# Recurrent mixer of a two-block model: head by head with the projections in between, instead of stage by stage

## The reference

```python
def hgrn2_mixer(x, lb, w_in, out_norm, w_o):
    proj = x @ w_in                                   # 1024 -> 4096
    q = silu(proj[..., :1024]); f = proj[..., 1024:2048]
    v = proj[..., 2048:3072];   gate = proj[..., 3072:]
    log_f = logaddexp(log(lb), log1p(-lb) + log_sigmoid(f))
    k = (1.0 - lb) * sigmoid(-f)
    # 8 heads of 128, chunks of 64 tokens; G = cumsum of log_f inside a chunk
    def step(state, chunk):
        inter = einsum('bhtd,bhde->bhte', qc * exp(G), state)
        decay = exp(where(causal, G[t] - G[s], -inf))
        A = einsum('bhtd,bhsd,bhtsd->bhts', qc, kc, decay)
        intra = einsum('bhts,bhse->bhte', A, vc)
        new_state = exp(G_last) * state + einsum('bhsd,bhse->bhde', kc * exp(G_last - G), vc)
        return new_state, inter + intra
    o = rms_norm_2(o, out_norm.reshape(H, DV))        # per head
    return (o * silu(gate)) @ w_o
```

## Time and profile before

| what | value |
| --- | --- |
| median of 3 runs | 3634.28 us (3632.82 to 18645.5) |
| the profiled execution's own time | 3637.17 us |
| its span, first to last instruction | 3635.4 us |
| PE busy | 3467.8 us (95%) |
| DVE, ACT, POOL busy | 1756.2 (48%), 754.0 (21%), 1944.4 us (53%) |
| mean granted PE clock | 0.969 |

### The profile page before, as it was taken

The page is one execution under the profiler, slowest core; times in us unless marked ns, Lnnn a source line. Parts: engine busy times, 40 slices in busy tenths (PEclk is TensorE's granted clock), DMA queues, the critical chain, the costliest instruction groups (busy, mean ns, idle before and its releaser), DMA issues. The chain is left out here.

```text
span 3635.4 us, 45543 instructions
## 1 busy us (share of the span) xinstructions
PE 3467.8 (95%) x15768; PEld 2738.6 (75%) x15768; DVE 1756.2 (48%) x3022; ACT 754.0 (21%) x1292; POOL 1944.4 (53%) x1172
## 2 busy tenths in 40 slices
PE   8998999999999999999999788899989999899998
PEld 4635788888888888888888556688767888588885
DVE  1043167768595657777775333423022856433203
ACT  2122122211112211111111232322022332222103
POOL 3403564555545566666666413466645652366663
PEclk9998999999999999999999979999999999899999
DMA  4431233535444475555554101222312200122231
GB/s 177 147 116 46 87 122 119 217 119 194 144 152 181 149 281 193 190 198 195 190 188 146 58 24 41 75 95 96 104 69 81 93 30 7 52 90 95 98 101 61
DMA packets 141137, 438.20 MB, mean 121 GB/s; under 512 B 13568, under 2 KB 13696, under 8 KB 136832
## 3 DMA queue, kind: packets, MB, share of 16 engines
q1 hardware_dynamic: 82512, 301.62, 24.2%
q10 hardware_dynamic: 58544, 135.55, 10.6%
HBM read 367.91 MB, written 69.21 MB: 120 GB/s over the span
## 5 line engine op out<-in xcount | busy, mean ns | idle before, releaser
L1757 POOL TENSOR_SCALAR whi<-ring 128x1024 fp32r<-128x1024 f32 x519 | 563.8, 1086 | 1585.8 <-issue 942.9
L1759 POOL TENSOR_TENSOR wlo<-ring,whi 128x1024 fp32r<-128x1024 f32 x519 | 1310.1, 2524 | 43.4
L364 PE MATMUL ps<-norm_hi,whi 128*128 128x512 f32 x1304 | 556.8, 427 | 14.1 <-DVE norm_lo L1186 13.0
L366 PE MATMUL ps<-norm_hi,wlo 128*128 128x512 f32 x1304 | 512.6, 393 | 0.0
L365 PE MATMUL ps<-norm_lo,whi 128*128 128x512 f32 x1304 | 511.0, 392 | 0.0
L364 PE MATMUL ps<-mixed_hi,whi 128*128 128x512 f32 x1024 | 398.4, 389 | 2.7 <-DVE mixed_lo L1488 2.7
L366 PE MATMUL ps<-mixed_hi,wlo 128*128 128x512 f32 x1024 | 398.4, 389 | 0.0
L365 PE MATMUL ps<-mixed_lo,whi 128*128 128x512 f32 x1024 | 398.3, 389 | 0.0
L1484 DVE TENSOR_TENSOR A<-A 128x512 f32<-128x512 f32 x128 | 353.9, 2765 | 22.8 <-DMA A<-gate_map 21.9
L364 PE MATMUL ps<-mix_hi,whi 128*128 128x512 f32 x768 | 303.7, 395 | 18.8 <-DVE mix_lo L1186 18.8
L365 PE MATMUL ps<-mix_lo,whi 128*128 128x512 f32 x768 | 302.1, 393 | 0.0
(11 more groups left out here) (332 smaller groups left out, 5231.8 us busy)
## 6 DMA issues: line engine op xcount, KB each, us to landing
ring<-stream SPq DMA_DIRECT2D x519, 512.0 KB, 3.3
gelu_map<-A ACTq DMA_DIRECT2D x128, 256.0 KB, 2.0
gate_map<-A ACTq DMA_DIRECT2D x16, 2048.0 KB, 11.7
A<-gelu_map ACTq DMA_DIRECT2D x128, 256.0 KB, 3.3
A<-gate_map ACTq DMA_DIRECT2D x32, 1024.0 KB, 6.0
A<-ada_w SPq DMA_DIRECT2D x12, 2048.0 KB, 8.2
X<-x_in SPq DMA_DIRECT2D x1, 2048.0 KB, 17.8
out<-X SPq DMA_DIRECT2D x8, 256.0 KB, 2.0
```

The lines of the kernel that those rows point to most:

```text
L364: first = mm(out_, lh, rh, start=start, stop=False)
L366: return first, mm(out_, ll, rh, start=False, stop=stop)
L1757: g.tensor_scalar(h[:], raw[:], 1.0, 0.0, ALU.mult, ALU.add).then_inc(whi_ready, 1)
L1759: g.tensor_tensor(rest[:], raw[:], h[:].bitcast(F32), ALU.subtract).then_inc(split_ready, 1)
```

## The change

The layer is rewritten as a loop over heads with three heads in flight. Turn i has the projections of head a = i, the pairs and states of head b = i-1, the output and norm of head c = i-2, and the gating of head d = i-3. A turn has eight slots on PE. In each stands half a product of head a, in the order forget gate, value, output gate, query, two slots for each; the weight columns are laid out to match. Values are now projected by feature and transposed on PE, like the decayed keys, both through bank 2.

The pairs of one head are no longer multiplied with the values level by level. DVE writes those of level 0 masked into a plane and merges those of the other levels and of the diagonal into the same plane by `copy_predicated`; then PE multiplies the plane with the values once per head. The states of a head are kept side by side (7 updates in a row, each waiting for the one before), and their products with the decayed queries are accumulated in the same bank, so that the addition on DVE is gone. The norm is made per head with a full sum by `ones`, a root and a reciprocal over 128x512, and no spread. POOL makes the gaps of a head between its splits. Planes, semaphores and the norm's bookkeeping follow (`HE` now has 12 buffers for the gaps; most others have two, by the parity of the head).

The core of the diff:

```diff
 # tensor
-            linear("hgrn_in", "x_hgrn", count=16)
-            by_token("hgrn_v", "x_hgrn", KC, PROD["hgrn_in"] + 16)
-            linear("hgrn_in", "x_hgrn", tiles="hgrn_gate", first=24, count=8)
...
+            def hgrn_linear(h, s):
+                part, half = divmod(s, 2)
+                t, p = FIRST["hgrn"] + 4 * h + part, PROD["hgrn"] + 4 * h + part
+                for k in range(4 * half, 4 * half + 4):
+                    if k == 0:
+                        tile_in(t)
+                        pe.wait_ge(bank_free, p + 1)
...
+            def hgrn_delta(h, odd):
+                if h:
+                    pe.wait_ge(state_ready, (NCH - 1) * h)
+                for c in range(odd, NCH - 1, 2):
...
+                    last = mm(ps[:, 3 + 2 * odd, w], A[r, HKT, w], A[r, HV + h % 2, w], start=True, stop=True)
+                last.then_inc(delta_ready, 1)
+            def hgrn_out(h):
+                pe.wait_ge(masked_ready, (LEVELS + 1) * (h + 1))
...
+                    mm(ps[:, 4, r], two(HV, h)[:, r], two(HMASK, h)[:, r], start=tb == 0, stop=False,
+                       skip_group_check=True)
+                for c in range(1, NCH):
+                    pe.wait_ge(state_ready, (NCH - 1) * h + c)
+                    r = slice(c * CH, (c + 1) * CH)
+                    last = mm(ps[:, 4, r], states(h, c - 1), two(HLF, h)[:, r], start=False, stop=c == NCH - 1,
+                              skip_group_check=True)
...
+            for i in range(HEADS + 2):
+                a, b, c = i, i - 1, i - 2
+                for s in range(SLOTS):
+                    if a < HEADS:
+                        hgrn_linear(a, s)
+                    if c >= 0:
+                        if s == 0:
+                            hgrn_out(c)
+                        if s == 2:
+                            pe.wait_ge(hsq_ready, c + 1)
...
+                            mm(ps[:, 2, :], ones[:], plane(HSQ), start=True, stop=True).then_inc(hsum_ready, 1)
+                    if 0 <= b < HEADS:
+                        if s == 0:
+                            pe.wait_ge(khat_ready, b + 1)
...
+                            hgrn_turn(2, plane(HKH)).then_inc(kt_ready, 1)
+                        if s == 1:
...
+                            hgrn_turn(2, plane(HVF)).then_inc(vt_ready, 1)
+                        if s == 2:
+                            pe.wait_ge(vt_taken, b + 1)
+                            hgrn_delta(b, 0)
+                            hgrn_delta(b, 1)
+                        if s >= 1:
+                            hgrn_pairs(b, s - 1)
 # scalar
+            for i in range(HEADS + 3):
+                a, b, c, d = i, i - 1, i - 2, i - 3
+                if 0 <= b < HEADS:
...
+                    take("hgrn", 4 * b + QUERY, two(HQ, b), ACT.Silu)
...
+                    fn(plane(HKT), ps[:, 2, :], ACT.Copy).then_inc(kt_taken, 1)
+                if 0 <= c < HEADS:
...
+                    fn(two(HO, c), ps[:, 4, :], ACT.Copy)
...
+                    fn(plane(HSQ), ps[:, 4, :], ACT.Square).then_inc(hsq_ready, 1)
...
+                if a < HEADS:
...
+                    fn(two(HLF, a), ps[:, p % 2, :], ACT.Sigmoid)
+                    fn(two(HK, a), ps[:, p % 2, :], ACT.Sigmoid, scale=-1.0).then_inc(bank_free, 1)
+                if 0 <= c < HEADS:
...
+                    fn(plane(HRS), ps[:, 2, :], ACT.Sqrt, scale=1.0 / P, bias=eps_col[1e-6]).then_inc(hroot_ready, 1)
+                if a < HEADS:
+                    act.wait_ge(forget_in, a + 1)
+                    fn(two(HLF, a), two(HLF, a), ACT.Ln).then_inc(log_ready, 1)
...
+                    take("hgrn", 4 * a + VALUE, plane(HVF))
+                    act.wait_ge(cum_ready, a + 1)
+                    fn(two(HLF, a), two(HG, a), ACT.Exp).then_inc(decay_ready, 1)
+                    act.wait_ge(decay_in, a + 1)
+                    fn(plane(HKH), plane(HKH), ACT.Exp).then_inc(decay_ready, 1)
...
+                    fn(dec[:, a, :], ends, ACT.Exp).then_inc(decay_ready, 1)
+                    for lv in range(LEVELS):
+                        e = a * LEVELS + lv
+                        act.wait_ge(gap_ready, e + 1)
+                        x = plane(HE + e % (2 * LEVELS))
+                        fn(x, x, ACT.Exp).then_inc(gap_exp, 1)
+                    if a >= 2:
+                        act.wait_ge(gated_ready, a - 1)
+                    take("hgrn", 4 * a + OUT_GATE, two(HGT, a), ACT.Silu)
 # vector
+            def keep_pairs(h, lv):
...
+                if lv == 0:
...
+                    ins = v.tensor_tensor(kept, pairs, mask.unsqueeze(1).broadcast_to([P, TB, P]), ALU.mult)
+                else:
+                    dve.wait_ge(masked_ready, u)
+                    ins = v.copy_predicated(kept, mask.bitcast(U32).unsqueeze(1).broadcast_to([P, TB, P]), pairs)
...
+            for i in range(HEADS + 3):
+                a, b, c, d = i, i - 1, i - 2, i - 3
...
+                    gate_output(d)
+                if 0 <= b < HEADS:
+                    make_level(b, 0)
+                    make_level(b, 1)
+                    decayed_query(b)
...
+                    low("o_hgrn", d, two(HO, d))
+                if 0 <= b < HEADS:
+                    keep_pairs(b, 0)
+                    make_level(b, 2)
+                    keep_pairs(b, 1)
+                    make_level(b, 3)
+                if a < HEADS:
+                    forget(a)
+                if 0 <= b < HEADS:
+                    keep_pairs(b, 2)
+                    make_level(b, 4)
+                    update_states(b, 0, 4)
+                    keep_pairs(b, 3)
+                    make_level(b, 5)
+                if a < HEADS:
+                    cumulate(a)
+                if 0 <= b < HEADS:
+                    keep_pairs(b, 4)
+                    update_states(b, 4, 7)
+                if a < HEADS:
+                    to_end(a)
+                if 0 <= b < HEADS:
+                    keep_pairs(b, 5)
+                if 0 <= c < HEADS:
+                    invert_root(c)
+                if 0 <= b < HEADS:
+                    keep_pairs(b, 6)
+                if 0 <= c < HEADS:
+                    normed(c)
+                if a < HEADS:
+                    decayed_key(a)
 # gpsimd
             for h in range(HEADS):
...
+                n = FIRST["hgrn"] + 4 * h + 2
+                split(n % RING, n)
+                split((n + 1) % RING, n + 1)
+                pool.wait_ge(cum_ready, h + 1)
+                if h >= 2:
+                    pool.wait_ge(level_ready, LEVELS * (h - 1))
+                for lv in range(3):
+                    gaps(h, lv)
+                split((n + 2) % RING, n + 2)
+                for lv in range(3, LEVELS):
+                    gaps(h, lv)
+                split((n + 3) % RING, n + 3)
```

More of the change, by code:

```diff
@@ L321, in build, with two, states @@
         TMPO, CENTER, SG, UU, TMPD, TMPG, TMPP, PRAW = 40, 56, 16, 18, 0, 40, 48, 66
-        HQ, HLF, HK, HV, HGT, HG, HKH, HKT, HO, HM, HE, HMASK = 16, 24, 32, 40, 48, 56, 64, 8, 64, 72, 0, 4
-        STATES = [A[:, first:first + 2, :].rearrange("p a t -> p (a t)").rearrange("p (h e) -> p h e", h=HEADS)
-                  for first in (6, 4)]
+        HQ, HLF, HK, HVF, HG, HKH, HKT, HV, HGT, HE, HM, HMASK = 16, 18, 20, 22, 24, 26, 27, 28, 30, 32, 44, 46
+        HSTATE, HO, HSQ, HRS = 48, 52, 54, 55
+        FORGET, VALUE, OUT_GATE, QUERY = range(4)
+        SLOTS = 8
+        def two(first, h):
+            return plane(first + h % 2)
+        def states(h, c):
+            first = HSTATE + 2 * (h % 2) + c // 4
+            return A[:, first, c % 4 * P:c % 4 * P + P]
         def hi(name, j):
@@ L426, in linear @@
                 elif loops > 1:
-                    if p0 in EASED:
-                        some(t0, p0, 0, per, EASED)
-                    with pe.Fori(int(p0 in EASED), loops) as i:
+                    with pe.Fori(0, loops) as i:
                         some(t0, p0, i, per)
@@ L1614, in _, with by_level, by_block, forget @@
             ffn_and_ple(0)
-            for h in range(HEADS):
-                taken("hgrn_in", 8 + h)
-                lf = plane(HLF + h)
+            def by_level(ap, lv):
+                return ap.rearrange("p (b two m) -> p b two m", two=2, m=2 ** lv)
+            def by_block(ap):
+                return ap.rearrange("p (b t) -> p b t", b=TB)
+            def forget(h):
+                taken("hgrn", 4 * h + FORGET)
+                lf, k = two(HLF, h), two(HK, h)
                 own.do(v.tensor_scalar(lf, lf, small[:, OMLB + h:OMLB + h + 1], small[:, LB + h:LB + h + 1], ALU.mult,
@@ L1628, in _, with to_end @@
                     .then_inc(cum_ready, 1)
+            def to_end(h):
                 dve.wait_ge(cum_ready, h + 1)
[L1630 to L1637 removed]
@@ L1644, in make_level, with decayed_key, decayed_query @@
+            def decayed_key(h):
+                dve.wait_ge(decay_ready, 3 * h + 2)
```

(33 more changed lines are left out.)

278 lines of the change are left out of this document (116 added, 162 removed).

## The result

The changed kernel takes 3651.26 us (median), the kernel before 3636.11 us in the same series: 1.0045 times the time, 95% interval 1.003 to 1.0059. It is slower by about 15 us, which is within the 2% that count as no change. The forecast was 3643 us, no change. The profiled execution took 3650.54 us, against 3637.17.

The account below looks back on a forecast made before the run. TensorE, busy 95% of the span, bounds the kernel; stalled turns of 44.0 us and a bare tail add 8.5 us to the profiled 3637.17, giving 3645.7; the median 2.9 lower gives 3643 us, range 3595 to 3696.

Parts of the forecast that it names:

- TensorE's work: One turn of the new loop: projections, pairs, states and output take TensorE 34.5 us if it never waits.
- Turn 0: First turn, projections alone: cumulative sum at about 2773 us, slot 0 of turn 1 starts at 2787.
- The queue order: Each turn's end: output gate's take waits behind scan, gaps, split and Exps, so TensorE idles 7.6 us.
- VectorE's work: VectorE's whole turn: about 21 us of work, not the bound by its sum.
- The prices: Rowless predicated copies taken at 0.61 us, bounds 0.61 and 1.22; reciprocals 3.35 us each, costed at nothing in the loop.
- The clock: Behind each idle stretch, some 3.7 us of TensorE's work runs at half clock, losing 1.9 us.
- The turn: Loop turn with stall and clock loss: 44.0 us, turn 1 40.5; six full turns end at 3091.5.
- the tail: After the loop: some 17 us of VectorE's work to 3109.5, then 13.6 us to the first hgrn_o product at 3123.
- A: Rival: output gate's take isn't late, turns of 34.5 us, 3577 us; chance 0.1 for gains of 40 us or more.
- B: Rival: VectorE and POOL block each other more, +7.5 us a turn, 3696 us; chance 0.2 for half or more.
- C: Rival: half clock through slots 0 and 1 plus half of B, turns of 50.8 us, 3691 us; chance 0.07.
- D: Rival: projections and mixing don't overlap, so the old sum stands at 3634 us; no chance given.

Follow-up runs that it names:

- kernel 10: Changed kernel with the output gate's take before the sum, POOL's split before the gaps and the first state updates before level 4: 3593.05 us.
- kernel 1: Changed kernel with ScalarE's take of the output gate moved before its wait for the cumulative sum, using a third gate plane: 3595.96 us.
- kernel 9: Changed kernel with 38 spare 128x128 matmuls on TensorE in the stall at the start of turns 1 to 7: 3642.95 us.
- kernel 2: Changed kernel with POOL's split of the next forget tile moved before its wait for the cumulative sum, ahead of all gaps: 3657.61 us.
- kernel 8: Kernel before, not interleaved, with seven masked products per head replaced by six predicated copies and one product: 3626.35 us, 0.997 of the time before.
- kernel 5: Changed kernel with VectorE's first four state updates of a head moved before level 4: 3653.83 us.
- kernel 4: Changed kernel with two spare ScalarE copies of 0.6 us right before the table load and the output gate's take: 3669.13 us.
- kernel 6: Changed kernel with 30 spare 128x128 matmuls on TensorE in the stall at the start of turns 1 to 7: 3649.25 us.

## Why the prediction was right

The verdict and the time held (3651.26, in the range and within the forecast's own 3622 to 3664), and by the mechanism that was named. That the number came so close is in part luck, since steps that were off cancel. By its steps, in absolute time of the profiled executions:

- **TensorE's work** of 34.5 us a turn: at full clock and without stalls kernel 10's turn is 35.2 to 35.4 with 0.8 to 1 us of waits left. Right.
- **Turn 0**: the gaps start at 2773.00 us (forecast: about 2773), and slot 0 of turn 1 at 2786.74 (forecast: 2787). The sum itself was there at 2769.4, earlier than forecast, but a split stood before the gaps until then. The agreement is luck: the layer began 2.7 us earlier than before (2745.57 for 2748.26), which no step foresaw, and from there to slot 0 of turn 1 it took 41.2 us where the sum has 38.7. The sum also started from a misread row: 2764.19 is the last block of the first product, and the second begins at 2765.22, 1.0 us later (ScalarE takes the first at 2765.42).
- **The queue order**: idle 7.65 to 8.69 us, seven times, released by ScalarE's take (forecast: 7 or 8, by Silu). POOL does wait for the scan. `make_level(b,4)` did meet the split: 2.59 us. Right. Its pieces, from the start of slot 0 at 2871.50 us, with the clock's 1.9 us added to the forecast: the sum at 29.4 us (30.2), POOL's gaps, split and gaps 12.4 us (11.0), from there to slot 0 of the next turn 2.7 (2.8).
- **VectorE's work** was put at 21 us a turn, and it is busy 29.6 (177.64 in six turns). The main part is the meetings: three levels of each turn meet a split, and their second halves take 2.6 us each instead of 0.42. It cost nothing here, since VectorE waits anyway; in kernel 1 it is busy 163.9 of 214 us.
- **The prices.** A predicated copy has 734 ns in its row and 0.62 us from start to start (forecast: 0.61); this timeline of DVE in the changed kernel shows that, and the reciprocal (L1757) that ran beside POOL's split of 2904.97 without a loss on either side: 3.34 us here, 3.36 alone, and the split 1.05 and 2.35.

```profile
2903.76 0.75 DVE L1738 COPY_PREDICATED A<-level_mask,ps 128x512 f32<-128x512 uint32 x1 [0.50 <-PE ps L763]
2904.40 3.34 DVE L1757 RECIPROCAL A<-A 128x512 f32<-128x512 f32 x1
2907.65 0.68 DVE L1738 COPY_PREDICATED A<-ident,ps 128x512 f32<-128x512 uint32 x1
```

  The rule of the Trainium skill (SBUF — State Buffer, Who interferes with whom) that only instructions of VectorE with two SBUF inputs or in a two-port mode lock POOL out agrees with that: the level, with two SBUF inputs, went from 0.42 to 2.59 us beside the split, while the reciprocal, with one, kept its 3.34.
- **The table load**: 2914.00 + 1.28, and the take at 2915.30. No row shows a drain of 1.4 us (the Trainium skill, ScalarE: Activation LUTs, What ACT_TABLE_LOAD costs), and the turn is at the time without it, so the trace decided rightly here.
- **The clock**: 1.9 us a turn forecast, 1.5 in the rows (4.36 against 2.84) and 1.5 by kernel 9. About right.
- **The turn**: 44.0 forecast, 44.4 measured. From the start of turn 1 to that of turn 8 the sum gave 304.5 us, and it took 307.0: +2.5.
- **The step that was mis-sized: the tail**, 13.6 + 17 and a take, 31.5 us in the sum from 3091.5 on. From the take it took 36.8 us (from 0.75 us behind it, where a turn starts, 36.1: +4.6). I had called it "VectorE's own work" and let TensorE be ready. The timelines of the changed kernel show it isn't. Of VectorE:

```profile
3098.50 0.42 DVE L1724 TENSOR_TENSOR A<-A 128x256 f32<-128x256 f32 x1
3102.22 0.73 DVE L1738 COPY_PREDICATED A<-level_mask,ps 128x512 f32<-128x512 uint32 x1 [3.30 <-PE ps L763]
```

  And of TensorE:

```profile
3095.57 1.92 PE L763 MATMUL ps<-A 128*128 128x128 f32 x8
3097.28 1.91 PE L804 MATMUL ps<-A,ones 128*128 128x512 f32 x2
3099.12 1.98 PE L773 MATMUL ps<-A 64*128 64x128 f32 x14
3101.03 2.05 PE L763 MATMUL ps<-A 128*128 128x128 f32 x16
...
3113.64 1.88 PE L783 MATMUL ps<-A 128*128 128x128 f32 x8 [4.03 <-DVE A L1738]
3115.31 3.09 PE L788 MATMUL ps<-A 128*128 128x64 f32 x14
```

  The pairs that VectorE wants stand in TensorE's queue behind other pairs (3095.57), the sum of the head before (L804) and the deltas (L773), and these ran mostly at half clock (0.57 from 3093 to 3101 us): eight 128x128 matmuls took 1.92 us here, 1.05 in the loop (2906.30). That is 3.3 us of waiting. From 3093.72 to the output's start at 3113.64 it took 19.9 us, where the sum has 18.0. The output (L783, L788) again runs at half clock behind 4.03 us of idle time, and so does the sum behind it (L804, 2.08 us): from the output to the take it took 16.2 us, where the sum has 13.6.
- **Behind the take** I had added 1.9 us for a product at half clock. It isn't there: the clock was back at 0.99 from 3124 us on, before the take. Summed, -0.3 (turn 0) + 2.5 + 4.6 - 1.9 = +4.9 us, which is the profiled 3650.54 against the 3645.7 of the sum. The -0.3 is itself -2.7 (the earlier start) and +2.4. The median missed by more, 3651.26 for 3643: the forecast took it 2.9 us under the profiled execution, and it lies 0.7 above.

Of the rivals, A (the gate in time) is kernel 1: forecast 3577 us and turns of 34.5, found 3596 and 35.6. It isn't what the change does, but it is what the change could have been. Its 3577 us was 19 us short: turns of 35.6 instead of 34.5 us are 8 of them, and the rest isn't assigned. B was wrong in that a half of the gaps took 0.75 us on average (L1883 0.78, L1884 0.73, of 96 in all), with the levels beside some of them, and the reciprocal blocks nobody; what it had right is the 1.4 us by which POOL's part is longer. C was wrong in that the clock recovers within one half product. D was wrong in that projections and pairs do alternate on TensorE (L376 to L378 and L763, up to 2906.30); that the layer is no shorter than before has another cause.

## What to carry to other kernels

When work of several engines is interleaved by hand, follow each queue to the instruction that frees the accumulator bank of the bound engine: one take behind a chain that it doesn't need cost 8.4 us in each of seven turns, and moving it turned +0.45% into -1.2%. Check what else the moved step waits for: this one also needed a third plane. Before moving a step into another engine's idle stretch, look at when its operands and slots come free, not only at when the engine is (kernel 2). Removing work from TensorE alone pays only down to the next engine's sum (kernel 8: 12 of 37 us), and the tail of a pipelined loop must be costed as a chain of its own, through every queue in it.

## What the runs showed of the hardware

- The price of a stall of TensorE is not its length alone, and it doesn't grow evenly. Behind 8.69 us of idle time the half product took 4.31 to 4.44 us, behind 7.66 us it took up to 5.26 (kernel 5), behind 8.4 to 8.6 us 4.6 to 5.0 (kernel 2), at 2.82 to 2.86 without. So 1.0 us won in the queue gave little, and 1.1 us lost cost up to 2.2 (kernel 4). What decides how long the clock stays at 0.50 after work resumes isn't settled.
- The clock also fell behind an idle stretch of only 2.00 us, and not in it but about 1 us after work had resumed (kernel 6: 1.00 at 2908 to 2910, 0.62 and 0.52 after). One turn earlier the same kernel idled for 2.02 us and the clock stayed at 1.00, and so it did behind 1.16 us, six times (kernel 1), and behind 0.2 us (kernel 9).
- A predicated copy with its operand in PSUM and a broadcast mask costs nearly the same as a plain masking multiply: 0.73 and 0.68 us in the rows, 0.6 from start to start.
- A VectorE instruction with two SBUF inputs that meets a POOL split stretches by up to 2.2 us (0.42 to 2.6 for a half level of 128x256, 21 times in the changed kernel); a reciprocal (3.34 us), a predicated copy and a state update beside a split keep their own price.
